# Block 1 of a PEER layer taken out ahead of blocks 2 and 3, and three weight loads put in front of the gather rows

## The chip, the cores and the metric

The kernel runs on one core of a Trainium2 chip. The metric is device microseconds of one execution. TensorE (PE) multiplies, VectorE (DVE) and ScalarE (ACT) work on elements, GpSimd (POOL) issues the indirect gathers, SyncE (SP) issues all plain loads and stores, and 16 DMA engines move the data.

## The reference

One decoder layer over 512 tokens of width 1024, in float32:

```python
z = x @ w_in      # q, fz, iv, og, cb, cc, ch, ga, gb, 1024 columns each
yc = cb * causal_depthwise_conv3(cc * ch, conv_w, conv_b)
merged = jax.nn.sigmoid(ga) * (o @ w_branch_a) + jax.nn.sigmoid(gb) * (yc @ w_branch_b)
x = layer_norm(ALPHA * x + merged @ w_out, ln1_g, ln1_b)
# peer(x): per token and head (8): product-key search, 16 experts of 16384
qh = (xb @ w_q).reshape(tb, PK_HEADS, 2, PK_HALF)
s = jnp.einsum('thpd,hpkd->thpk', qh, sub_keys)
s1, i1 = lax.top_k(s[:, :, 0], 16); s2, i2 = lax.top_k(s[:, :, 1], 16)
top, pos = lax.top_k(cand, 16)      # cand: the 256 sums of s1 and s2
h = gelu(einsum('thkd,td->thk', u[eidx], xb)); out = einsum('thk,thkd->td', softmax(top) * h, v[eidx])
x = layer_norm(ALPHA * x + out, ln2_g, ln2_b)
x = x + jax.nn.sigmoid(x @ ple_w_gate) * (p @ ple_w_proj)
```

Here o is a chunkwise gated recurrence over 8 heads. The 128 chosen experts of a token (8 heads by 16) are 8 KB each, u and v side by side.

## The kernel before, in words

The tokens are four blocks of 128. A first stage computes the recurrence for all of them and takes block 0 alone as far as its PEER queries. Then follow 512 **rows**, 128 to a block: row r gathers one expert of each of the 128 tokens (1 MB), VectorE multiplies its u half with x (dot, L1596), ScalarE makes the coefficient (gelu, softmax weight), and the v half is added with that coefficient, either by TensorE through a diagonal matrix into PSUM (`sum_v`, L2111) or, in the rows of the list SHARED, by VectorE (L1609). Six buffers `uv` hold gathered rows, a seventh is added from row MERGE_R to the end of block 0, two more from QUERY_R on. GpSimd issues the gather of a row when the row that had its buffer is summed.

The rest of the layer for blocks 1 to 3 is put into the rows of block 0 by tables of row numbers that each engine's program reads (`tail_row`):

- 40 **units** of 128 columns of x @ w_in (L2011; CHH, CC, CB for the convolution, GA, GB for the gates); two units share one 1 MB load, a pair. UNIT_ROW spreads them.
- 16 **merges** (L2030 and by VectorE L1358, L1363) with `w_branch_a` and `w_branch_b`, by MERGE_ROW.
- 12 **outs** (L2044, residual L1371) with `w_out`, by OUT_ROW, then the first norm of each block (L1378, L1385, L1395) by NORM_ROW and the transposes by TURN_ROW.
- the **queries** of 8 heads (L2078) and their **scores** (L2092), for blocks 1 to 3 in one product of 384 columns, by QUERY_ROW and SCORE_ROW.
- the **search** of an item (a block and a head, 15 steps on VectorE). Item i must be done before row 16 i is gathered. Item 8 is the first of block 1.

Every engine works through its own program in order; waits are on semaphores. Weights go by SP's queue, in order, into 1 MB slots: `raw` 0 to 3, `raw_w` 4 and 5. In the rows, units, merges and outs rotate over slots 0, 1, 2, and a load waits until the product that read its slot has ended. PSUM banks rotate over four for units and merges, so that TensorE can be four of them ahead of the engine that reads them.

A block's end (second norm, gate product L2161, projection L2176, store) runs in the rows of the next block, from FIN_TURN on. After row 511 comes a short tail.

Of the kernel before, what the change touches and what calls it, by code (L numbers as in the profile page):

```python
# [32 lines left out]
def build(nc, x, x_t, p_t, w_a, w_in, vec_cols, w_branch_a, w_branch_b, w_out,  # L33
# [21 lines left out]
    with ctx:  # L55
# [35 lines left out]
        def slot(i):  # L91

            if i < 4:
                return raw[:, i]
            if i < 6:
                return raw_w[:, i - 4]
            return raw_y[:, i - 6] if i < 8 else raw_g[:, i - 8]
# [132 lines left out]
        raw_in = [sem(f"raw_in{i}") for i in range(12)]  # L230
# [52 lines left out]
        def search_rows(i):  # L283

            if i == 1:
                return [k // 3 for k in range(STEPS)]
            if i == PKH:
                return [SCORE_ROW[0] + 2 + k // 2 for k in range(STEPS)]
            return [TOPK * (i - 2) + TOPK // 2 + k for k in range(STEPS)]

        UNITS = [(sect, 2 * cp + i) for cp in range(KT // 2) for sect in (6, 5, 4) for i in range(2)]
# [6 lines left out]
        UNIT_ROW += [[(UNIT_MM * n + i) * 58 // (UNIT_MM * (len(UNITS) - EARLY)) for i in range(UNIT_MM)]  # L298
                     for n in range(len(UNITS) - EARLY)]
        UNIT_ROW[EARLY] = [-1] + UNIT_ROW[EARLY][1:]  # L300
        UNIT_END = [rows[-1] for rows in UNIT_ROW]
        MERGE_ROW = [58 + n * 23 // 128 for n in range(16 * KT)]
        OUT_ROW = [83 + n * 11 // 96 for n in range(4 * (TB - 1) * KT)]
        NORM_ROW = [None] + [OUT_ROW[-1] + 1 + 2 * b for b in range(1, TB)]
        TURN_ROW = [None] + [NORM_ROW[b] + 3 for b in range(1, TB)]
        Q0 = TURN_ROW[-1] + 2
        QUERY_ROW = [[Q0 + (n * 5 // 16 if h == 0 else 6 + n * 6 // 16 if h == 1 else 17 + 14 * (h - 2) + n * 9 // 16)
                      for n in range(2 * KT)] for h in range(PKH)]
        SCORE_ROW = [QUERY_ROW[h][-1] + 2 for h in range(PKH)]

        SEARCH = [(i, search_rows(i)) for i in range(1, ITEMS)]

        def shared(r):

            b, k = divmod(r, BLOCK_ROWS)
            if b == 0:
                if r <= OUT_ROW[-1] + 3:
                    return True
                return r % 3 == 1 and 106 <= r <= 120
# [23 lines left out]
        MERGE_R, QUERY_R = BLOCK_ROWS - 2 - 5 * (UV + 1), QUERY_ROW[-1][-1] + 11  # L343
# [31 lines left out]
        FIN_TURN = 5  # L375
        FIN_GATE = [8 + n for n in range(2 * KT)]
        FIN_P = [FIN_GATE[-1] + 2 + n for n in range(4)]
# [43 lines left out]
        LOADS += [(("unit", n), n - 2 if n < 4 else (n - 2) % 3) for n in range(2, len(UNITS) // 2)]  # L421
        LOADS += [(("merge", m), m % 3) for m in range(8)]
        LOADS += [(("out", c), (c + 2) % 3) for c in range(4)]
        LOADS += [(("query", 1, h), h % 2) for h in range(PKH)]
# [7 lines left out]
        def blocks(pc):  # L432
            return range(*PIECES[pc])

# [40 lines left out]
        rest = [("merge", 1, c, i) for c in range(4) for i in range(4)]  # L475
        rest += [("out", 1, c, b) for c in range(4) for b in blocks(1)]
        rest += [("turn", 1, b, kh) for b in blocks(1) for kh in range(2)]
        for n, name in enumerate(rest):
            use(4 + (n + 2) % 4, *name)
        for h in range(PKH):  # L480
            for i in range(4):
                use(4 + i % 2, "query", 1, h, i)
# [42 lines left out]
        def chunk_end(m):  # L525
# [3 lines left out]
            return USE["out", 1, m - 8, TB - 1] + 1  # L529


        @block.sync
        def _(sp):
# [65 lines left out]
            sp.wait_ge(t_done, USE["unit", 1] + 1)  # L599
            unit_fetch(2)  # L600
            for h in (3, 4, 5):
                sp.wait_ge(t_done, USE["query", 0, h - 3, 1] + 1)
                fetch(pk_w_q[h], "query", 0, h)
            sp.wait_ge(t_done, USE["unit", 3] + 1)
            unit_fetch(3)
# [11 lines left out]
            for n in range(4, len(UNITS) // 2):  # L617
                if n == 4:
                    sp.wait_ge(t_done, USE["query", 0, 5, 1] + 1)
                elif n < 7:  # L620
                    sp.wait_ge(t_done, USE["unit", 2 * (n - 3) + 1] + 1)
                else:
                    sp.wait_ge(t_done, USE["unit", 2 * (n - 3) + 1] + 1)
# [6 lines left out]
            def tail_fetch(m, src, *name):  # L630
                if m < 3:
                    sp.wait_ge(t_done, USE["unit", len(UNITS) - 5 + 2 * m] + 1)
                else:
                    sp.wait_ge(t_done, chunk_end(m - 3))
# [7 lines left out]
            def query_fetch(h):  # L642
                if h < 2:
                    sp.wait_ge(t_done, chunk_end(9 + h))
                else:
                    sp.wait_ge(t_done, USE["query", 1, h - 2, 1] + 1)
# [10 lines left out]

            query_fetch(0)
            query_fetch(1)
            sp.wait_ge(t_done, chunk_end(11))  # L660
            sp.dma_start(w_ple[:], ple_w_proj).then_inc(ple_in, 16)

            sp.wait_ge(x1_done, TB)
            sp.dma_start(w_gate[:], ple_w_gate).then_inc(gate_in, 16)
            query_fetch(2)
            query_fetch(3)
# [58 lines left out]
        def _(act):  # L725
# [206 lines left out]
            def query_out(pc, h, parts=range(4)):  # L932
                bs = blocks(pc)
                n = P * len(bs)
                for i in parts:
# [3 lines left out]
                    o = qhT[pc][:, i, 0:n] if i < 2 else scores[:, i - 2, h, bs[0] * P:bs[0] * P + n]  # L939
# [54 lines left out]
            def tail_row(r):  # L994
# [13 lines left out]
                for h in range(PKH):  # L1008
                    for a in range(2):
                        if r == QUERY_ROW[h][KT * a + KT - 1] + 1:  # L1010
                            query_out(1, h, [a])
                    if r == SCORE_ROW[h] + 1:
                        query_out(1, h, [2, 3])
# [48 lines left out]
            for r in range(ROWS):  # L1062
# [8 lines left out]
                if b >= 0:  # L1071
                    if k == 2:
                        root_of(b, x2_var, x2_root)
                    if k == FIN_TURN + 1:
                        x2_turn_out(b)
                    if k == FIN_GATE[-1] + 1:
# [1266 lines left out]
```

## Time and profile before

| | us |
|---|---|
| median of 3 runs | 1784.62 (1783.69 to 1786.54) |
| the profiled execution, its own time | 1783.85 |
| its span | 1781.9 |
| TensorE busy | 1572.8 (88%) |
| VectorE busy | 1321.1 (74%) |
| ScalarE busy | 778.3 (44%) |
| GpSimd busy | 497.4 (28%) |
| DMA | 655.40 MB |

The profiled execution's time is 1.95 us more than its span, and 0.77 us less than the median. Busy time is a mean over stages with different limits, so it doesn't say by itself which engine a stage waits for; a page also divides the span into 40 slices of 44.5 us, and windows of the trace give the same for any stretch. DMA share is the busy share of the 16 DMA engines, and can read a little over 1.

### The profile page before, as it was taken

Reading aid. Unit: us, or ns where it says so; the run is one execution under the profiler, and the core shown is the slowest. Engines: PE = TensorE matmul, PEld = TensorE weight load, DVE = VectorE, ACT = ScalarE, POOL = GpSimd, SP = SyncE. Lnnn points to the kernel's source line nnn. Section 1 sums busy time; section 2 is a strip of 40 time slices with the busy share of each in tenths; the row PEclk is TensorE's granted clock in tenths of the full one; section 3 lists DMA queues with packets and bytes.
Section 4 is the critical chain, followed back from the end, with each engine's and each line's share of the span. In section 5 each row is a group of like instructions: output and inputs, shape, how many; then the busy total and the mean of one; then the engine's idle time right before and its main releaser. Section 6 shows DMA issues by size and latency. Waiting matters only on the chain. (4 is left out here: it accounts for less than half of the span.)

```text
span 1781.9 us, 16998 instructions
## 1 busy us (share of the span) xinstructions
PE 1572.8 (88%) x5000; PEld 874.4 (49%) x5000; DVE 1321.1 (74%) x2804; ACT 778.3 (44%) x1937; POOL 497.4 (28%) x528
## 2 busy tenths in 40 slices
PE   8999999999999997989888668788898878787778
PEld 7888888766655575544344223333333323222224
DVE  4454588599888999678878886886666687766666
ACT  6567695422222224343334334444444443444453
POOL 0000000122222232324333443333333333333331
PEclk9999999999999999999999999999999999999999
DMA  5113289799999999999999999999999999999994
GB/s 205 70 70 141 94 317 402 281 421 421 397 419 421 422 406 404 424 417 421 421 415 415 421 421 422 420 422 421 421 421 422 419 408 422 422 419 421 422 410 179
DMA packets 94933, 655.40 MB, mean 368 GB/s; under 512 B 10368, under 2 KB 14208, under 8 KB 17152
## 3 DMA queue, kind: packets, MB, share of 16 engines
q0 software_dynamic: 73728, 536.90, 72.8%
q1 hardware_dynamic: 20832, 116.97, 16.7%
q8 instruction: 37, 0.61, 0.1%
q10 hardware_dynamic: 288, 0.52, 0.1%
q14 instruction: 48, 0.39, 0.1%
HBM read 652.26 MB, written 2.10 MB: 367 GB/s over the span
## 5 line engine op out<-in xcount | busy, mean ns | idle before, releaser
L2111 PE MATMUL psum<-uv,diag 128*128 128x512 f32 x1424 | 707.3, 627 | 193.3 <-ACT diag L991 189.9
L720 POOL DMA_INDIRECT uv<-in_pk_uv,idx x512 | 495.0, 967 | 1249.6 <-PE psum L2111 563.9
L1596 DVE CUSTOM_DVE_ANT_0 uv<-uv,psum 128x1024 f32<-128x1024 f32 x512 | 622.9, 1217 | 295.1 <-DMA uv<-in_pk_uv,idx 288.0
L2111 PEld LDWEIGHTS psum<-uv,diag 128*128 128x128 f32 x1424 | 257.7, 194 | 613.2 <-ACT diag L991 389.7
L979 ACT ACTIVATE gelu<-dots 128x1 f32<-128x1 f32 x512 | 103.5, 202 | 764.1 <-DVE dots L1596 761.9
L2011 PE MATMUL psum<-xT,raw 128*128 128x384 f32 x640 | 208.4, 486 | 0.0
L1609 DVE SCALAR_TENSOR_TENSOR oT<-uv,coef,oT 128x1024 f32<-128x1024 f32 x151 | 193.3, 1280 | 4.2 <-ACT coef L983 4.2
L2011 PEld LDWEIGHTS psum<-xT,raw 128*128 128x128 f32 x640 | 120.7, 190 | 81.7
L983 ACT ACTIVATE coef<-gelu,weight 128x1 f32<-128x1 f32 x512 | 150.8, 295 | 16.6
L991 ACT ACTIVATE diag<-ident,coef 128x128 f32<-128x128 f32 x356 | 143.0, 402 | 11.6
L1847 PE MATMUL psum<-xTh,w_hi 128*128 128x512 f32 x248 | 98.6, 398 | 0.0
L1847 PE MATMUL psum<-xTl,w_hi 128*128 128x512 f32 x248 | 96.8, 390 | 0.0
L1847 PE MATMUL psum<-xTh,w_lo 128*128 128x512 f32 x248 | 96.5, 389 | 0.0
L2078 PE MATMUL psum<-oT,raw 128*128 128x384 f32 x256 | 92.2, 491 | 0.0
L1118 DVE TENSOR_TENSOR w_lo<-raw_a,w_hi 128x1024 fp32r<-128x1024 f32 x32 | 39.2, 1225 | 69.9 <-ACT w_hi L735 69.6
L2078 PEld LDWEIGHTS psum<-oT,raw 128*128 128x128 f32 x256 | 49.1, 192 | 45.6 <-issue 25.7
L1847 PEld LDWEIGHTS psum<-xTl,w_hi 128*128 128x128 f32 x248 | 46.5, 188 | 10.1
L1847 PEld LDWEIGHTS psum<-xTh,w_lo 128*128 128x128 f32 x248 | 46.6, 188 | 9.1
L1847 PEld LDWEIGHTS psum<-xTh,w_hi 128*128 128x128 f32 x248 | 46.6, 188 | 8.9
L2161 PE MATMUL psum<-w_gate,x2T 128*128 128x512 f32 x96 | 47.9, 592 | 0.0
L735 ACT ACTIVATE w_hi<-raw_a 128x1024 fp32r<-128x1024 f32 x32 | 34.0, 1061 | 31.3 <-PE psum L1847 27.9
L979 ACT ACT_TABLE_LOAD x35 | 44.9, 1283 | 0.6
(284 smaller groups left out, 1722.5 us busy)
## 6 DMA issues: line engine op xcount, KB each, us to landing
raw<-in_w_in SPq DMA_DIRECT2D x32, 1024.0 KB, 8.9
raw_a<-in_w_a SPq DMA_DIRECT2D x12, 1024.0 KB, 4.8
raw<-in_pk_w_q SPq DMA_DIRECT2D x10, 1024.0 KB, 9.5
raw_y<-in_w_in SPq DMA_DIRECT2D x8, 1024.0 KB, 6.8
raw<-in_w_branch_a SPq DMA_DIRECT2D x8, 1024.0 KB, 7.7
uv<-in_pk_uv,idx POOLq DMA_INDIRECT x512, 14.6
raw<-in_w_out SPq DMA_DIRECT2D x6, 1024.0 KB, 9.6
raw_w<-in_pk_w_q SPq DMA_DIRECT2D x6, 1024.0 KB, 9.5
```

Source lines behind the costliest of these rows:

```text
L720: pool.indirect_dma_start(row_uv(r)[:], None, pk_uv, bass.IndirectOffsetOnAxis(idx[:, i % 2, j:j + 1], 0)).then_inc(row_loaded(r)[0], 16)
L979: nc.scalar.activation(gelu[:, r % 4:r % 4 + 1], dots[:, r % 32:r % 32 + 1], ACT.Gelu).then_inc(gelu_done, 1)
L983: nc.scalar.activation(coef[:, r % 8:r % 8 + 1], gelu[:, r % 4:r % 4 + 1], ACT.Copy, scale=weight[:, i % 2, j:j + 1]).then_inc(coef_done, 1)
L991: nc.scalar.activation(diag[:, n % DR, :], ident[:], ACT.Copy, scale=coef[:, r % 8:r % 8 + 1]).then_inc(diag_done, 1)
L1118: V.tensor_tensor(w_lo[:, s], raw_a[:, slot, half], w_hi[:, s].bitcast(F32), ALU.subtract).then_inc(lo_done, 1)
L1596: V.tensor_tensor_reduce(u, u, x_cur[:], 1.0, 0.0, ALU.mult, ALU.add, dots[:, r % 32:r % 32 + 1]).then_inc(dot_done, 1)
L1609: V.scalar_tensor_tensor(out=acc, in0=v, scalar=c, in1=acc, op0=ALU.mult, op1=ALU.add).then_inc(acc_step, 1)
L1847: last = T.matmul(B[bk][:], w[:, s, k, :], xx[:, k, :], start=(k == 0 and i == 0), stop=(k == KT - 1 and i == 2))
L2011: last = T.matmul(B[bank(r)][:, 0:SEQ - P], slot(SLOT["unit", n // 2])[:, k, half * P:half * P + P], xT[:, k, P:], start=(k == 0), stop=(k ...
L2078: last = T.matmul(B[bank(r)][:, 0:n], w[:, k, a * P:a * P + P], turned[:, k, :], start=(k == 0), stop=(k == KT - 1), skip_group_check=True)
L2111: last = T.matmul(B[i][:], diag[:, n % DR, :], row_uv(r)[:, D + i * 512:D + (i + 1) * 512], start=(r in FIRST), stop=last_of_block, skip_g ...
L2161: last = T.matmul(B[6 + i][:], x2T[:, k, :], w_gate[:, k, i * 512:(i + 1) * 512], start=(k == 0), stop=(k == KT - 1), skip_group_check=True)
```

## The change

Five things are done in one edit. (1) Three slots, 12 to 14, are laid over columns that stand free for a time: those of blocks 2 and 3 in the first scores, and two blocks' columns in gaT and gbT. A load into such a slot is eight separate runs of 256 columns in each partition. Pairs 2, 3 and 4 are loaded there ahead of the rows, and slot 12 stays in the rotation to the end of outs. (2) Units take rows 0 to 67 where they took 0 to 57, merges 68 to 92 (58 to 80). (3) Outs are done for block 1 first, its norm in rows 101 to 103, then for blocks 2 and 3, with norms in rows 115 to 119; before, three norms stood in rows 96 to 102. (4) Queries 0 and 1 are computed for block 1 in rows 106 to 113 and for blocks 2 and 3 in rows 122 to 131; the other six stay joint. Item 8 is searched in rows 112 to 119 (113 to 120 before), item 10 in rows 143 to 150 (136 to 150). (5) SHARED has rows 0 to 112 in block 0 (0 to 96, 106, 109, 112, 115 and 118 before); the seventh buffer starts at row 105 (91); block 0's end starts 16 rows later.

```diff
+            if i >= 12:
+                return (scores[:, 0, :, 2 * P:], gaT[:, :, P:P + CW], gbT[:, :, P:P + CW])[i - 12]
...
             if i == PKH:
-                return [SCORE_ROW[0] + 2 + k // 2 for k in range(STEPS)]
+                return [SCORE_ROW[1, 0] + 2 + k // 2 for k in range(STEPS)]
+            if i == PKH + SPLIT:
+                return [SCORE_ROW[1, SPLIT] + 2 + k // 2 for k in range(STEPS)]
...
+        SPLIT = 2
+        MERGE0 = 68
-        UNIT_ROW += [[(UNIT_MM * n + i) * 58 // (UNIT_MM * (len(UNITS) - EARLY)) for i in range(UNIT_MM)]
+        UNIT_ROW += [[(UNIT_MM * n + i) * MERGE0 // (UNIT_MM * (len(UNITS) - EARLY)) for i in range(UNIT_MM)]
...
-        MERGE_ROW = [58 + n * 23 // 128 for n in range(16 * KT)]
+        MERGE_ROW = [MERGE0 + n * 25 // 128 for n in range(16 * KT)]
+        OUT0 = MERGE_ROW[-1] + 2
+        OUTS = [(c, 1) for c in range(4)] + [(c, b) for c in range(4) for b in range(2, TB)]
...
+        LATER = [(1, h) for h in range(SPLIT)] + [(2, h) for h in range(SPLIT)] + [(1, h) for h in range(SPLIT, PKH)]
...
-                if r <= OUT_ROW[-1] + 3:
-                    return True
-                return r % 3 == 1 and 106 <= r <= 120
+                return r <= OUT_ROW[-1]
...
-        MERGE_R, QUERY_R = BLOCK_ROWS - 2 - 5 * (UV + 1), QUERY_ROW[-1][-1] + 11
+        MERGE_R, QUERY_R = BLOCK_ROWS - 2 - 3 * (UV + 1), QUERY_ROW[1, PKH - 1][-1] + 11
...
-        FIN_TURN = 5
+        FIN_TURN = [21] + [5] * (TB - 1)
...
-        LOADS += [(("unit", n), n - 2 if n < 4 else (n - 2) % 3) for n in range(2, len(UNITS) // 2)]
-        LOADS += [(("merge", m), m % 3) for m in range(8)]
+        RING = (0, 1, 2, 12)
+        AHEAD = (12, 13, 14)
+        LOADS += [(("unit", n), (AHEAD + RING[:3] + AHEAD)[n - 2] if n < 11 else RING[(n - 11) % 4])
+                  for n in range(2, len(UNITS) // 2)]
+        LOADS += [(("merge", m), RING[(m + 1) % 4]) for m in range(8)]
...
             fetch(pk_w_q[2], "query", 0, 2)
-            sp.wait_ge(t_done, USE["unit", 1] + 1)
-            unit_fetch(2)
+            for n in range(2, 5):
+                unit_fetch(n)
             for h in (3, 4, 5):
                 sp.wait_ge(t_done, USE["query", 0, h - 3, 1] + 1)
                 fetch(pk_w_q[h], "query", 0, h)
+            sp.wait_ge(t_done, USE["unit", 1] + 1)
+            unit_fetch(5)
...
-            query_fetch(0)
-            query_fetch(1)
-            sp.wait_ge(t_done, chunk_end(11))
-            sp.dma_start(w_ple[:], ple_w_proj).then_inc(ple_in, 16)
-
+            for h in range(4):
+                query_fetch(h)
             sp.wait_ge(x1_done, TB)
             sp.dma_start(w_gate[:], ple_w_gate).then_inc(gate_in, 16)
-            query_fetch(2)
-            query_fetch(3)
+            sp.wait_ge(t_done, query_end(2, 1))
+            sp.dma_start(w_ple[:], ple_w_proj).then_inc(ple_in, 16)
             load_p(0)
```

On SP's queue the loads around the first gather stood like this before. keysT are the sub-keys, in_pk_w_q are query weights, in_w_in unit pairs, x2 two alike in a row; a load with 128x8x256 goes in runs of 256 columns.

```order
L597 DMA keysT<-in_sub_keys_t 128x2048 [waits zl_done]
L556 DMA raw<-in_pk_w_q 128x2048
L556 DMA raw<-in_w_in 128x2048 [waits t_done]
L556 DMA raw_w<-in_pk_w_q 128x2048 [waits t_done] x2
L556 DMA raw<-in_pk_w_q 128x2048 [waits t_done]
L556 DMA raw<-in_w_in 128x2048 [waits t_done]
```

In the changed kernel the same place of SP's queue reads:

```order
L632 DMA keysT<-in_sub_keys_t 128x2048 [waits zl_done]
L591 DMA raw<-in_pk_w_q 128x2048
L591 DMA scores<-in_w_in 128x8x256
L591 DMA gaT<-in_w_in 128x8x256
L591 DMA gbT<-in_w_in 128x8x256
L591 DMA raw_w<-in_pk_w_q 128x2048 [waits t_done] x2
L591 DMA raw<-in_pk_w_q 128x2048 [waits t_done]
L591 DMA raw<-in_w_in 128x2048 [waits t_done] x2
```

Three unit pairs have moved ahead of the waits on t_done, and the query loads no longer stand behind the wait for unit 1.

On VectorE, row 101 of the kernel before holds a dot (ISA, two instructions), one step of item 7's search (sel, weight), and the second step of block 3's first norm (BN_AGGR and the pass over x_sb).

```order
L1596 ISA uv_124,dots<-uv_124,psum 128x1024
L1596 ISA dots 128x1
L1509 TENSOR_REDUCE sel<-hot 128x16
L1511 TENSOR_REDUCE sel<-cand 128x16
L1515 TENSOR_SCALAR weight<-top_e,e_rec 128x16
L1383 BN_AGGR mean_var<-stats 128x2
L1385 SCALAR_TENSOR_TENSOR x_sb<-x_sb,mean_var,gaT 128x1024
```

The same norm step stands in row 118 of the changed kernel, behind two steps of item 8's search:

```order
L1629 ISA uv_123,dots<-uv_123,psum 128x1024
L1629 ISA dots 128x1
L1535 TENSOR_TENSOR hot<-hot,best_i 128x256
L1537 TENSOR_TENSOR cand<-cand,best_i 128x256
L1539 RECIPROCAL e_rec<-e_sum 128x1
L1542 TENSOR_REDUCE sel<-hot 128x16
L1544 TENSOR_REDUCE sel<-cand 128x16
L1548 TENSOR_SCALAR weight<-top_e,e_rec 128x16
L1416 BN_AGGR mean_var<-stats 128x2
L1418 SCALAR_TENSOR_TENSOR x_sb<-x_sb,mean_var,gaT 128x1024
```

The norms of blocks 2 and 3 have moved 17 rows later, from rows with one step of a search to rows with two.

## Rows read from the trace of the kernel before

**Rows 1.** The page: GB/s by slice, and the gathers' queue.
```profile
GB/s 205 70 70 141 94 317 402 281 421 421 397 419 421 422 406 404 424 417 421 421 415 415 421 421 422 420 422 421 421 421 422 419 408 422 422 419 421 422 410 179
...
q0 software_dynamic: 73728, 536.90, 72.8%
```

**Rows 2.** Windows: us, busy PE, PEld, DVE, ACT, POOL, PEclk, DMA share, GB/s.
```profile
345.00:455.00 110.00, 108.73 (x455) 72.07 (x454) 97.50 (x202) 27.93 (x98) 26.15 (x27) 1.00 1.01 419
455.00:475.00 20.00, 20.00 (x64) 11.79 (x63) 17.81 (x34) 3.18 (x13) 4.70 (x5) 1.00 0.97 378
475.00:645.00 170.00, 169.77 (x527) 99.72 (x525) 154.86 (x296) 42.43 (x132) 48.44 (x51) 1.00 1.01 421
645.00:705.00 60.00, 51.08 (x215) 40.32 (x216) 57.72 (x116) 19.62 (x50) 18.33 (x19) 0.97 1.01 410
705.00:730.00 25.00, 21.82 (x67) 10.89 (x66) 15.66 (x28) 11.87 (x31) 7.52 (x8) 1.00 0.97 396
```

**Rows 3.** Windows around the first gather, same columns.
```profile
326.00:336.00 10.00, 9.56 (x58) 7.51 (x57) 5.34 (x18) 4.04 (x12) 0.00 (x0) 1.00 0.04 16
336.00:342.00 6.00, 5.76 (x52) 5.60 (x51) 5.25 (x26) 2.32 (x5) 4.13 (x4) 1.00 0.96 363
```

**Rows 4.** Windows of rows 0 to 102, L1596 alone: busy us (two instructions a row).
```profile
347.40:541.00 193.60, 65.85 (x108) 1.00 1.01 415
541.00:641.30 100.30, 35.42 (x58) 1.00 1.01 421
641.30:679.50 38.20, 14.63 (x24) 1.00 1.00 403
679.50:711.40 31.90, 9.74 (x16) 0.95 0.99 406
```

**Rows 5.** Timeline of VectorE in rows 30, 88 and 98.
```profile
464.21 0.56 DVE L1329 TENSOR_TENSOR u_pad<-u_pad,psum 128x384 f32<-128x384 f32 x1 [2.11 <-PE psum L2011]
...
657.49 1.21 DVE L1596 CUSTOM_DVE_ANT_0 uv<-uv,psum 128x1024 f32<-128x1024 f32 x1
...
658.63 1.28 DVE L1609 SCALAR_TENSOR_TENSOR oT<-uv,coef,oT 128x1024 f32<-128x1024 f32 x1
659.83 0.48 DVE L1456 MAX8 best<-scores 128x8 f32<-128x128 f32 x2
660.23 0.40 DVE L1371 SCALAR_TENSOR_TENSOR x_sb<-x_sb,psum 128x256 f32<-128x256 f32 x1
660.55 1.21 DVE L1596 CUSTOM_DVE_ANT_0 uv<-uv,psum 128x1024 f32<-128x1024 f32 x1
...
695.16 1.28 DVE L1395 SCALAR_TENSOR_TENSOR x_sb<-x_sb,rstd,gbT 128x1024 f32<-128x1024 f32 x1
```

**Rows 6.** Timeline of SP's issues, of the first gather and the first dot.
```profile
335.31 0.33 SPq L556 DMA_DIRECT2D raw<-in_w_in  x1
335.68 4.17 SPq L556 DMA_DIRECT2D raw_w<-in_pk_w_q  x2
...
364.42 0.33 SPq L556 DMA_DIRECT2D raw<-in_w_in  x1
...
336.66 1.09 POOL L720 DMA_INDIRECT uv<-in_pk_uv,idx  x1 [333.40 <-DVE idx L1561]
...
347.43 1.22 DVE L1596 CUSTOM_DVE_ANT_0 uv<-uv,psum 128x1024 f32<-128x1024 f32 x1 [4.48 <-DMA uv<-in_pk_uv,idx]
```

**Rows 7.** Windows: xT alone (1.5 KB pieces), ln1 alone (512 B), gathers alone (8 KB).
```profile
296.00:298.00 2.00, 2.00 (x11) 1.65 (x10) 0.73 (x2) 1.10 (x2) 0.00 (x0) 1.00 1.06 372
309.00:311.00 2.00, 2.00 (x8) 1.18 (x7) 2.00 (x4) 0.33 (x1) 0.00 (x0) 1.00 1.18 292
1000.00:1200.00 200.00, 150.03 (x307) 56.16 (x308) 155.29 (x366) 83.61 (x251) 77.05 (x79) 0.96 1.01 421
```

**Rows 8.** DMA issues of 540:580 and of 700:712: size, median us to landing.
```profile
uv<-in_pk_uv,idx POOLq DMA_INDIRECT x12, 13.4
...
uv<-in_pk_uv,idx POOLq DMA_INDIRECT x3, 6.1
```

## What I expect, and why

> **What bounds the kernel now.** I read the page first, from the stage of rows to the end. From slice 9 to slice 39 the DMA moves 397 to 424 GB/s in every slice, and 536.90 MB of it are gathers [rows 1]. A row's gather is 1 MB: at the 421 GB/s of the stretch 1000 to 1200 us [rows 7] it takes 1.0486/421 = 2.49 us, and that is what a row costs where nothing else is loaded. The reader is to see that after 350 us the DMA engines are full nearly all the time, whatever VectorE or TensorE do, so the end moves only with (a) megabytes that leave the stage of rows, (b) megabytes that cost more, and (c) time in which the DMA runs dry.
>
> The second view, the windows of the stage, shows where it runs dry [rows 2]. What is lost in a window is its length times (421 - GB/s)/421: 0.5 us in 345:455, 2.0 us in 455:475, 0 in 475:645, 1.6 us in 645:705, 1.5 us in 705:730. The third view, windows of 326 to 342 us, shows the idle just ahead of the first gather: 16 GB/s from 326 to 336 [rows 3]. The fourth is what TensorE and VectorE did. L1596 counts two instructions a row, so 54 rows took 193.6 us (3.59 us each), the next 29 took 3.46 us, 12 rows 3.18 us and 8 rows 3.99 us [rows 4]. TensorE was busy for 108.73 of 110, 20.00 of 20 and 169.77 of 170 us up to 645 [rows 2]. VectorE waits for TensorE there too, 2.11 us at 464.21 [rows 5]. So in units and merges TensorE is level with the DMA, and at 455:475 it is behind.
>
> **Step 1, loads ahead of the rows (a gain).** Before, the load of unit pair 2 was issued at 335.31 and that of query 3 at 335.68; pair 3 came at 364.42 and pair 4 behind it [rows 6]. Now pairs 2, 3 and 4 are issued right behind query 2 with no wait, before the DMA falls idle at 326, and query 3, which stood behind a wait for unit 1, comes when query 0's product ends, about 332.3 us. The three take 9.0 us (step 2 has the rate), from 326.3 to about 335.3; query 3 follows to 337.8. Nothing of the rows waits for them: the first gather is issued at 336.66, when VectorE has its indices. But the windows say that 363 GB/s were moved from 336 to 342 before, 2.2 MB, which is pair 2 and query 3 [rows 3]: those two were hidden in part already. After the change the stretch from 337.8 to about 341 is nearly empty, since the gathers' own data come late (issued 336.66, the first used at 347.43 [rows 6]). So of four loads (4.19 MB, 10.0 us) some 1.6 MB is given back: 2.6 MB at 421 GB/s, **-6.2 us**. Ends: 4.9 us, if only pairs 3 and 4 count, and 7.5 us, if only one load's worth is given back.
>
> **Step 2, the new columns (a loss).** Slots 12 to 14 hold eight pieces of 256 columns a partition, not one run of 8 KB: each load into them is 1,024 pieces of 1 KB. Eleven loads go there, three ahead of the rows and eight among them (pairs 8, 9, 10, 14, 18, merges 2 and 6, out 2). The trace has no full load in 1 KB pieces, but xT goes in pieces of 1.5 KB and ran at 372 GB/s, the two vectors of ln1 in pieces of 512 B at 292 GB/s, against 421 for 8 KB [rows 7]. By these, 16 engines spend 66 ns on 1.5 KB and 28 ns on 512 B, so 47 ns on 1 KB: 349 GB/s, 3.00 us a load, 0.52 us more than 2.49. Eight of them: **+4.1 us**. Ends: 2.6 us (0.33 each, at 372) and 8.8 us (1.1 each, at 292); 1 KB is nearer to the first.
> The Trainium skill, "DMA: Bandwidth & Descriptors", its table at the head, gives 512 B or more as the size from which a transfer runs at line rate; by that rule this term would be 0. The rows disagree, 292 and 372 GB/s at a full DMA share, and I go by them.
>
> **Step 3, ten more rows for units and merges (a gain).** In 475:645 TensorE issues 527 instructions in 169.77 us [rows 2], nearly all halves of a product of 384 columns: 0.322 us each, 16 to a unit or a merge, 5.15 us. 38 units over 58 rows are 3.38 us a row, over 68 rows 2.88 us; 16 merges over 23 rows 3.58 us, over 25 rows 3.30 us. The DMA asks per row for 2.49 us of gather plus pairs: 18 over 58 rows was 3.26 us, now 15 over 68 (five of them at 3.00) is 3.08 us. So TensorE, which asked for more than the DMA before, asks for less. The wait of 2.11 us for a unit, and the 2.5 us lost in 345:475, should go: **-2.4 us** (ends 0 and 2.5). In these rows VectorE has 1.14 + 1.20 us of dot and sum, 0.5 of search (below) and less of the units' work than before; it stays under the DMA's 3.08.
>
> **Step 4, VectorE at the end of the block (no change taken).** Rows 97 to 105, 107, 108, 110 and 111 are now summed by VectorE, 115 and 118 by TensorE: 11 sums of 1.20 us more on VectorE. Its steps, from the pitches in the timeline [rows 5]: dot 1.14, sum 1.20, residual 0.32; a block's norm is three passes over 1,024 columns of 1.28 each and two short instructions, 4.1 us. 3.18 us a row of 641.3:679.5 less 1.14, 1.20 and 0.32 leaves 0.52 of search, 8.3 for an item's 16 rows. Rows 95 to 100: 6 x 3.18 = 19.1. Rows 101 to 103, with block 1's norm: 9.5 + 4.1 = 13.6. Rows 104 to 111, no search in them: 8 x 2.34 + 5 x 0.32 = 20.3. Rows 112 to 119, where item 8 is searched at two steps a row and the norms of blocks 2 and 3 stand as well: 8 dots, 2 sums, the item, 2 residuals, 2 norms, 9.1 + 2.4 + 8.3 + 0.6 + 8.2 = 28.6. Together 81.6 us for 25 rows. The DMA has 25 gathers and three query loads in that time, 62.2 + 7.4 = 69.6, because the 4 MB gate load now stands on SP behind query 3, which waits for row 125. VectorE is 12.0 us too slow. What covers it is the backlog: a gather takes a median 13.4 us from issue to landing at 540:580 and 6.1 us at 700:712 [rows 8], so some 7 us can be used up before the engines starve, and the seventh row buffer (from row 105) gives one more load, 2.5 us, and the wider pitch of rows itself holds more in flight. Before, the 8 rows with three norms did the same (31.9 us against 22.4 of DMA), and 1.6 + 1.5 us were lost. I take the same 3.1 us again: **0**. Ends: 2 us less, and 12.0 us more (no cover at all).
>
> **Step 5, the rest, at nothing.** Queries 0 and 1 are done for block 1 (128 columns) and again for blocks 2 and 3 (256): same columns, 32 more products, some 1.6 us of TensorE, behind a DMA that sets the pace of rows 106 to 133. Item 10 is searched in 8 rows, 143 to 150: 1.14 + 0.6 + 1.0 = 2.7 us against 2.49, 2 us in 8 rows, which the backlog covers. Block 0's last product moves 16 rows later, out of query 3 and into query 4's rows; store and query 7 follow it and are due at row 193. From there to slice 39 nothing changes: 408 to 422 GB/s by slice [rows 1]. The tail after the last row is the same code.
>
> **Sum.** -6.2 + 4.1 - 2.4 + 0 = -4.5 us. On the profiled execution's own 1783.85 that is 1779.4; the median shown, 1784.62, is 0.8 above it, and on that scale I predict 1780.1. A measurement tells about 0.2% (3.6 us) from no change, so this lies just outside.
>
> **Rivals.** (A) No measurable change: step 3's gain is not had, because idle follows late gathers elsewhere, or TensorE, now bound to the rows by four banks, waits in their place. -2.1, 1782.5. For it: the whole kernel lost only 6 us in this stage, and the net of steps 1 and 2 is small. (B) Slower: in rows 95 to 119 the DMA runs dry. Its price is 12.0 us less the cover c, so 1792.1 - c, and it ends over +0.2% where c is under 3.9 us, that is if the stretch is entered with the backlog already used up (gathers landing in under 10 us at row 95). Against it: the 13.6 us to 6.1 us of the rows before. (C) Pieces of 1 KB cost no more than 8 KB: step 2 falls away, -8.6 us, 1776.0. Against it the 372 GB/s. That is the page's rule named above. (D) The piece cost at its upper end, 8.8 us: +0.2, 1784.8, no change.
>
> **Numbers.** Forecast 0.44, C 0.08, A 0.28, D 0.05, B 0.15. So faster by over 0.2%: 0.52; within: 0.33; slower: 0.15. Range 1775 to 1788: from C's time and a little more, to B with 4 us of cover; what is beyond is under 2 in 10. The forecast's own range is 1777.5 to 1781.
>
> **What would show it.** Step 1: GB/s over 300 in 326:336, and fewer loads up to row 60. Step 2: GB/s under 421 at a full DMA share where a slot of scores, gaT or gbT is loaded. Step 3: 345:475 at 418 or more, TensorE's busy time under 100% in units. Step 4: gathers' time to landing not under 6 us in rows 95 to 125, and about 3 us lost there. I am wrong if that last stretch loses 6 us or more, or if TensorE's queue at the block's turn (queries of blocks 2 and 3 in rows 122 to 133) holds row buffers back.

## The result, and the profile after

The changed kernel takes 1800.09 us (median of 4 runs, 1798.33 to 1802.23), before 1785.53 beside it (1783.69 to 1786.54): ratio 1.008, 95% interval 1.0067 to 1.0092 (for the runs below the interval stands in brackets behind the ratio). It is 0.8% slower; I had said 1780.1 and 1775 to 1788. The span is 1796.4 against 1781.9, and 14.5 us is what has to be found.

The page of after, by slices of 44.9 us, beside [rows 1]:
```profile
span 1796.4 us, 17043 instructions
...
GB/s 211 69 62 140 108 324 397 352 417 410 414 416 417 416 415 379 400 354 355 421 380 421 422 420 423 420 422 421 421 422 421 422 393 421 421 421 421 421 418 185
```
The eighth slice (314 to 359 us) rises from 281 to 352; the 16th to 19th (674 to 853 us) and the 21st have 354 to 400, where before had 404 to 424. The gain is early; nearly all of the loss lies between 670 and 950 us. Windows of after (us, busy PE, PEld, DVE, ACT, POOL, PEclk, DMA share, GB/s), to set beside [rows 2, 3]:
```profile
326.00:336.00 10.00, 9.56 (x60) 7.73 (x59) 5.59 (x20) 4.04 (x12) 0.00 (x0) 1.00 1.08 362
336.00:342.00 6.00, 5.12 (x47) 4.96 (x46) 4.82 (x23) 2.08 (x5) 4.58 (x5) 1.00 0.93 342
345.00:475.00 130.00, 129.02 (x518) 84.34 (x519) 120.36 (x244) 35.87 (x123) 33.75 (x35) 1.00 1.02 415
475.00:645.00 170.00, 158.38 (x483) 91.71 (x482) 153.97 (x293) 40.05 (x130) 49.07 (x51) 0.99 1.02 416
645.00:705.00 60.00, 46.69 (x188) 36.08 (x187) 59.53 (x113) 14.25 (x42) 17.84 (x19) 0.89 1.00 392
705.00:780.00 75.00, 65.94 (x267) 43.48 (x266) 63.58 (x144) 34.35 (x97) 23.34 (x24) 0.98 0.99 397
780.00:860.00 80.00, 56.83 (x176) 32.14 (x175) 50.43 (x107) 27.18 (x78) 21.36 (x22) 0.85 0.88 352
860.00:950.00 90.00, 82.23 (x221) 39.89 (x221) 68.73 (x153) 34.54 (x104) 31.15 (x32) 0.98 0.99 401
950.00:1755.00 805.00, 650.61 (x1400) 250.85 (x1399) 584.61 (x1401) 349.99 (x1036) 309.02 (x321) 0.98 1.01 419
```
The same stretches of before, where [rows 2] doesn't have them:
```profile
296.00:345.00 49.00, 47.84 (x254) 38.28 (x253) 33.63 (x71) 24.33 (x43) 6.02 (x6) 1.00 0.76 282
345.00:475.00 130.00, 128.73 (x517) 83.86 (x516) 115.32 (x235) 31.12 (x110) 30.84 (x32) 1.00 1.01 413
...
705.00:780.00 75.00, 68.08 (x200) 34.63 (x199) 52.91 (x124) 32.42 (x92) 23.50 (x26) 0.98 1.00 413
780.00:860.00 80.00, 74.75 (x213) 37.19 (x212) 66.35 (x146) 34.94 (x100) 29.16 (x29) 1.00 1.01 419
860.00:950.00 90.00, 74.59 (x196) 36.88 (x195) 72.17 (x162) 34.63 (x106) 33.62 (x33) 0.92 1.01 414
950.00:1755.00 805.00, 647.74 (x1389) 247.97 (x1388) 579.93 (x1382) 350.55 (x1036) 305.07 (x318) 0.98 1.01 419
```
From 950 on the two are alike: all is decided before. The deepest hole is 780:860, and TensorE is idle there too (busy 56.83 of 80 us, at a granted clock of 0.85). The list of VectorE's waits names what is new in it; before, the third and fourth of these were 5.9 and 4.6 us, and the second didn't exist:
```profile
DVE uv L1629 <- DMA uv<-in_pk_uv,idx: 259.6, 304, 2.2
...
DVE rstd L1423 <- DMA ln_bias<-in_ln_b: 19.5, 1, 19.5
...
DVE uv L1629 <- ACT psum L1000: 13.9, 4, 10.1
DVE gate L1754 <- PE psum L2210: 10.2, 4, 5.5
```
VectorE's timeline around the 19.5 us: dot 132, then nothing until ln_bias has landed, then the second norm of block 0, then dot 133.
```profile
783.92 1.21 DVE L1629 CUSTOM_DVE_ANT_0 uv<-uv,psum 128x1024 f32<-128x1024 f32 x1
785.06 0.08 DVE L1629 DVE_READ_ACCUMULATOR2_ANT dots<- 128x1 f32 x1
804.65 0.16 DVE L1423 RECIPROCAL rstd<-rstd 128x1 f32<-128x1 f32 x1 [19.51 <-DMA ln_bias<-in_ln_b]
```
No row is summed in that time, so no buffer comes free, and GpSimd stands:
```profile
790.05 0.94 POOL L752 DMA_INDIRECT uv<-in_pk_uv,idx  x1 [3.68 <-PE psum L2145]
809.02 0.94 POOL L752 DMA_INDIRECT uv<-in_pk_uv,idx  x1 [18.03 <-DVE oT L1640]
```
Why is a 512 KB load late? SP's issues in the timeline of after (L702 is ln2_bias):
```profile
696.61 74.11 SPq L591 DMA_DIRECT2D raw<-in_pk_w_q  x4
770.76 0.43 SPq L696 DMA_DIRECT2D w_gate<-in_ple_w_gate  x1
791.53 0.33 SPq L698 DMA_DIRECT2D w_ple<-in_ple_w_proj  x1
791.91 0.43 SPq L691 DMA_DIRECT2D pT<-in_p_t  x1
792.38 0.43 SPq L702 DMA_DIRECT2D ln_bias<-in_ln_b  x1
```
The wait of SP that is new, in its list of waits (total, times, longest):
```profile
SPq L698 <- PE psum L2111: 20.3, 1, 20.3
```
SP's issues before:
```profile
711.54 0.33 SPq L664 DMA_DIRECT2D w_gate<-in_ple_w_gate  x1
733.92 21.58 SPq L556 DMA_DIRECT2D raw<-in_pk_w_q  x2
...
787.54 0.33 SPq L670 DMA_DIRECT2D ln_bias<-in_ln_b  x1
```
The change puts w_ple on SP behind a wait for query (2, 1), because its place is now query 1's slot. That query is 16 products in TensorE's stream of rows 128 to 131. It ends near 791, and ln2_bias, which waits only for block 0's sum, is queued behind it. Likewise the 4 MB of w_gate come 59 us later than before, behind query 3's wait for query (2, 0).

### The profile page after: what moved, and what is told of

The parts are those of the page before. It is cut to its first block and busy times, and to the rows that moved or that the text cites. A ratio compares the mean times of both kernels' runs of the same rounds, so it can differ in the third digit from the quotient of the medians.

```text
span 1796.4 us, 17043 instructions
## 1 busy us (share of the span) xinstructions
PE 1560.2 (87%) x5020; PEld 876.9 (49%) x5020; DVE 1332.5 (74%) x2815; ACT 773.8 (43%) x1934; POOL 497.1 (28%) x528
## 3 DMA queue, kind: packets, MB, share of 16 engines
q1 hardware_dynamic: 30688, 116.97, 16.9%
## 5 line engine op out<-in xcount | busy, mean ns | idle before, releaser
L2145 PE MATMUL psum<-uv,diag 128*128 128x512 f32 x1380 | 685.8, 627 | 196.1 <-ACT diag L1024 191.9
L2145 PEld LDWEIGHTS psum<-uv,diag 128*128 128x128 f32 x1380 | 248.5, 194 | 602.2 <-ACT diag L1024 390.5
L1642 DVE SCALAR_TENSOR_TENSOR oT<-uv,coef,oT 128x1024 f32<-128x1024 f32 x162 | 207.4, 1280 | 4.6 <-ACT coef L1016 4.6
L1024 ACT ACTIVATE diag<-ident,coef 128x128 f32<-128x128 f32 x345 | 138.5, 402 | 11.3
L2044 PE MATMUL psum<-xT,raw 128*128 128x384 f32 x384 | 127.6, 491 | 2.4 <-ACT gaT L955 2.4
L2044 PEld LDWEIGHTS psum<-xT,raw 128*128 128x128 f32 x384 | 73.1, 192 | 52.5 <-issue 4.9
L2111 PE MATMUL psum<-oT,raw 128*128 128x384 f32 (+2 forms) x320 | 91.5, 423 | 0.4 <-ACT scores L973 0.4
L2111 PEld LDWEIGHTS psum<-oT,raw 128*128 128x128 f32 x320 | 56.5, 191 | 39.7 <-issue 22.7
L2044 PE MATMUL psum<-xT,scores 128*128 128x384 f32 x128 | 42.7, 487 | 3.9 <-ACT gbT L955 3.9
```

Source lines behind the costliest of these rows:

```text
L1024: nc.scalar.activation(diag[:, n % DR, :], ident[:], ACT.Copy, scale=coef[:, r % 8:r % 8 + 1]).then_inc(diag_done, 1)
L1642: V.scalar_tensor_tensor(out=acc, in0=v, scalar=c, in1=acc, op0=ALU.mult, op1=ALU.add).then_inc(acc_step, 1)
L2044: last = T.matmul(B[bank(r)][:, 0:SEQ - P], slot(SLOT["unit", n // 2])[:, k, half * P:half * P + P], xT[:, k, P:], start=(k == 0), stop=(k ...
L2111: last = T.matmul(B[bank(r)][:, 0:n], w[:, k, a * P:a * P + P], turned[:, k, :], start=(k == 0), stop=(k == KT - 1), skip_group_check=True)
L2145: last = T.matmul(B[i][:], diag[:, n % DR, :], row_uv(r)[:, D + i * 512:D + (i + 1) * 512], start=(r in FIRST), stop=last_of_block, skip_g ...
```

## Experiments

Theory Q: the 14.5 us are SP's order at the block's turn. Rival T: they are TensorE's stream there (the split queries), and SP's order is a symptom.

**e1**, two items of SP exchanged:
```diff
+            sp.wait_ge(acc_out, 2)
+            sp.dma_start(ln2_bias[:], ln2_b[0].partition_broadcast(P)).then_inc(ln2_in, 16)
             sp.wait_ge(t_done, query_end(2, 1))
             sp.dma_start(w_ple[:], ple_w_proj).then_inc(ple_in, 16)
             load_p(0)
-            sp.wait_ge(acc_out, 2)
-            sp.dma_start(ln2_bias[:], ln2_b[0].partition_broadcast(P)).then_inc(ln2_in, 16)
```


> The changed kernel with two SP items exchanged: the wait for fin_sum(0) and the load of ln2_bias now stand ahead of the wait for query (2, 1) and the load of w_ple. Theory Q (SP's order): in the profile of after VectorE waits 19.5 us at row 132 for ln_bias, which lands at 804.6 because SP stood 20.3 us at the wait for query (2, 1); the wait vanishes, and the time falls from 1800.1 by 14 to 19 us, to 1781 to 1786. Rival T (TensorE's stream): what delays the block's turn is the 16 products of query (2, 1) in rows 128 to 131, and ln_bias was only the last of two late things; then the stall stays within a few us of where it is and the time is 1794 or more.

Measured 1787.84, ratio to before 1.0021 (1.0012 to 1.003), against after's 1.008: 0.59%, 10.5 us. T is out as the main cause, but Q as I put it was only part of it: I had said 14 to 19 us. The wait shrank from 19.5 to 11.0 us and didn't vanish; VectorE's and SP's timeline in e1:
```profile
795.06 0.16 DVE L1423 RECIPROCAL rstd<-rstd 128x1 f32<-128x1 f32 x1 [10.99 <-DMA ln_bias<-in_ln_b]
...
769.70 0.43 SPq L696 DMA_DIRECT2D w_gate<-in_ple_w_gate  x1
775.20 0.33 SPq L698 DMA_DIRECT2D ln_bias<-in_ln_b  x1
```
and its DMA issues (KB each, median us to landing):
```profile
w_gate<-in_ple_w_gate SPq DMA_DIRECT2D x1, 4096.0 KB, 21.6
...
ln_bias<-in_ln_b SPq DMA_DIRECT2D x1, 512.0 KB, 19.8
```
Issued 17 us earlier, it took 19.8 us to land (7.4 before), 5.5 us behind 4 MB of gate weights.

**e2**, the suspected cost alone, in the kernel before:
```diff
-            sp.wait_ge(t_done, chunk_end(11))
-            sp.dma_start(w_ple[:], ple_w_proj).then_inc(ple_in, 16)
...
             query_fetch(3)
+            sp.wait_ge(t_done, USE["query", 1, 2, 1] + 1)
+            sp.dma_start(w_ple[:], ple_w_proj).then_inc(ple_in, 16)
             load_p(0)
```


> The kernel before with the suspected cost alone put in: w_ple is loaded behind queries 2 and 3 and behind a wait for the end of the second half of query 2 (row 130), so that ln2_bias stands behind that wait too; nothing else is changed. Theory Q: in the profile of before ln_bias was issued at 787.5 and landed at 795.0, about when dot 132 began (794.9); row 130 is reached near 788 to 791, three small loads go first, and ln_bias lands at 800 to 804, which costs 4 to 9 us: 1789 to 1795. Rival T: SP's order there costs nothing by itself: 1785.5, within 2 us.

1793.88, ratio 1.0054 (1.0041 to 1.0068): 9.6 us (I had said 4 to 9) for w_ple moved behind three other loads and a wait, nothing else touched. Its rows, VectorE and SP:
```profile
807.68 0.16 DVE L1389 RECIPROCAL rstd<-rstd 128x1 f32<-128x1 f32 x1 [9.99 <-DMA ln_bias<-in_ln_b]
...
797.80 0.33 SPq L665 DMA_DIRECT2D w_ple<-in_ple_w_proj  x1
...
798.64 0.43 SPq L669 DMA_DIRECT2D ln_bias<-in_ln_b  x1
```

**e5**, e1 with the gate load ahead of query 3, and **e12**, after with this alone:
```diff
-            for h in range(4):
+            for h in range(3):
                 query_fetch(h)
             sp.wait_ge(x1_done, TB)
             sp.dma_start(w_gate[:], ple_w_gate).then_inc(gate_in, 16)
+            query_fetch(3)
```


> As e1 (1787.8), and the 4 MB load of w_gate stands ahead of query 3 on SP and not behind its wait for query (2, 0). In e1 w_gate was issued at 769.7 (before: 711.5) and ln_bias, issued 5.5 us behind it, took 19.8 us to land (before: 7.4), so that VectorE still waited 11.0 us for it at row 132. Theory G (the gate load's place): w_gate is issued near 745 to 750 and is over when ln_bias is issued at 775, which lands near 783; the 11.0 us go, and the time is 7 to 11 us under e1: 1777 to 1781, faster than before. Rival R (the lead cannot be kept): TensorE, which must finish its queue at the block's turn, makes VectorE wait in rows 128 to 172 for something else, and the time stays at 1785 or more.

> The changed kernel with only w_gate's load moved ahead of query 3; ln_bias still stands behind the wait for query (2, 1). Theory (the two placements are two stalls in series, the later one ends last): ln_bias is still issued near 792, and only its landing, 12.2 us after issue in after, gets shorter, to 7 to 9 us: 3 to 6 us under after, a ratio near 1.005. Rival: SP's two placements add, and it is 5 us better than after by itself and e1's 10 us more are independent; or it gives nothing, within 1.5 us of after (1.008).

e5: 1782.47, ratio 0.9988 (0.9979 to 0.9997), 0.33% or 5.9 us under e1 and just under before; I had expected 7 to 11. w_gate was issued at 749.3, ln_bias at 777.6, and the norm went on without a wait:
```profile
788.02 0.16 DVE L1424 RECIPROCAL rstd<-rstd 128x1 f32<-128x1 f32 x1
788.29 1.28 DVE L1429 SCALAR_TENSOR_TENSOR x<-x,rstd,ln_bias 128x1024 f32<-128x1024 f32 x1
```
e12: 1795.47, ratio 1.006, 3.6 us under after. ln2_bias, issued at 791.92, landed 8.7 us later and not 12.2, and VectorE waited 15.2 us for it and not 19.5. So moving the gate load gives 3.6 us where ln2_bias is still behind query (2, 1), and 5.9 where it isn't. Both make the same landing late: the wait by a late issue, the gate load in front by a long way from issue to landing.

**e3, e6, e7, e9**, the smaller waits of the block's turn. e3 is e1 with `FIN_TURN = [12]` for block 0. e6 is e5 with `or 121 <= r <= 126` in SHARED. e7 is e6, and e9 is e5, with fin_gate and fin_add three rows later (`FIN_P[b][2 * i + 1] + 4`, `FIN_P[b][3] + 5`).

> As e1, and the turn of block 0's gate at row 12 of block 1 and not 21, so that its gate's products stand in rows 143 to 158 and the four of w_ple in rows 160 to 163, between queries 4 and 5, and no longer in rows 169 to 172 beside query 5's. Theory: the 5.5 us at row 172 that VectorE waits for the product of w_ple are a loss of their own and go: 3 to 5 us under e1. Rival: row buffers or a later wait take them back, and the time is e1's within 1.5 us.

> As e5, and the six rows 121 to 126 are summed by VectorE and not by TensorE (6 x 1.72 us off TensorE's stream, 6 x 1.20 us onto VectorE's). In e1 dot 128 waited 9.0 us for ScalarE's copy of block 1's tokens, which stood behind the copy of query (2, 0), whose products TensorE reached 5 us late. Theory: that wait falls to under 2 us and half of it or more is kept: 3 to 6 us under e5. Rival: row buffers come free no earlier, the lead is bounded by the transfers, and the time is e5's within 1.5 us; or VectorE, at 2.9 us a row there, is slower than the 2.5 us in which a row arrives, and it is 1 to 3 us over e5.

> As e6, and VectorE's products of the gate with the projection (fin_gate, fin_add) stand three rows later in each block, so that VectorE goes on with dots where it stood 5.4 us in row 172 of e1 for the last product of w_ple. Theory: TensorE is late there only against VectorE's order, and 3 to 5 us go. Rival: TensorE is late by its own load in rows 150 to 173 (two gates' products, queries 4 and 5), row buffers wait for its sums instead, and the time is e6's within 1.5 us.

> As e5 (ratio 0.9988 to before), with fin_gate and fin_add three rows later in each block and without the six more shared rows of e6. In e5 dots fell back by 5.0 us against before at row 172, where VectorE waits for the product of w_ple. Theory: 1.5 to 4 us under e5 (1779 to 1781). Rival: e7 kept only 1.6 us of these 5, since row buffers then waited for TensorE's sums in rows 176 to 185, and so it is here: within 1.5 us of e5.

e3: 1787.6, ratio 1.0016 against e1's 1.0021: the rival. The wait moved to row 162 (6.11 us, for the same product). e6: 1785.11, 0.9999, 2.0 us over e5: the rival again. In e6 GpSimd stood 10.29 us for a sum of TensorE ahead of its gather at 781.14, and 780:860 moves 399 GB/s where e5 moves 419. e7: 1783.06, 0.999, 1.6 us under e6, just past its rival's 1.5 where the theory wanted 3 to 5. e9: 1782.06, 0.9985 (0.9976 to 0.9994), 0.5 us under e5, the rival. Dot 172 of e7 stands 6.4 us ahead of e6's and dot 185 only 1.8, since GpSimd waited for TensorE's sums between them. Four edits at the places where VectorE is seen to wait, and none worth 2 us. What I read from this, and no run shows by itself: in rows 140 to 185 TensorE holds this schedule (81 to 82 of 90 us busy in 860:950 in after and e5, 74.59 before, since block 0's products stand there), and who is seen to wait for it is only a matter of order.

**e4, e10, e14, e15**, what made the early lead. e4 is before with the three loads ahead, pair 5 on over the old three slots:
```diff
-        LOADS += [(("unit", n), n - 2 if n < 4 else (n - 2) % 3) for n in range(2, len(UNITS) // 2)]
+        LOADS += [(("unit", n), n + 10 if n < 5 else (n - 5) % 3) for n in range(2, len(UNITS) // 2)]
...
-            sp.wait_ge(t_done, USE["unit", 1] + 1)
-            unit_fetch(2)
+            for n in range(2, 5):
+                unit_fetch(n)
```
e10 is e4 with the change's AHEAD and RING. e14 has the rows of e5 (MERGE0 = 68, split queries) with no load ahead and three slots, out 3 alone in slot 12; e15 is e14 with the three loads ahead. Both also wait at the block's turn in another order than e5 (w_ple behind query (2, 0), and query 3 behind w_ple and query (2, 1)), so they are set against e5 up to 705 us only.

> The kernel before with only the three unit pairs loaded ahead of the rows, into the same places in 1 KB pieces (pairs 2 to 4); from pair 5 on a ring of the three old slots, the unit, merge and output rows as before, queries not split. By the forecast's first step it is 6.2 us faster less three loads' share of the 1 KB pieces (3 of 11, 1.1 us): 1780.4. By the trace of after, where row 0 came 3.9 us earlier: 1781.6. Rival: a lead at row 0 is given back where VectorE and not the DMA sets the pace (rows 95 to 119), and it ends within 1.5 us of before, 1784 to 1787.

> The kernel before with the three loads ahead and the change's ring of four places (the fourth a column of first scores) and six places for pairs 5 to 10, but none of the rest: units, merge and output rows, queries of three blocks, block 0's gate and SP's order at the block's turn as before. Theory M (the lead is made by loads and ring, and lost by the new order at the block's turn): dot 33 is 6 to 10 us earlier than in before, as in e5, and with SP's old order the lead stays: 4 to 8 us under before, a ratio of 0.9955 to 0.998. Rival N (the longer rows for units made the lead): TensorE or VectorE holds rows 8 to 58 at their old pace, as in e4, and it is within 2 us of before.

> The other half of e10: no unit pair loaded ahead and the old ring of three places (the fourth output chunk alone stands in the free column of first scores, since the new output order needs four at once), but unit, merge and output rows, the split queries and the order of e5 as in e5. Theory P (the loads make room and the longer rows let it be used: neither alone gives the lead): dot 33 stands within 2 us of before and the time is at or over before, 1784 to 1789. Rival N (the longer rows made the lead by themselves, since TensorE was busy 160.00 of 160 us in 400:560 of before): dot 33 is 4 us or more earlier, and the time is e5's within 2 us.

> As e14, with the three pairs loaded ahead again (into the columns, 1 KB pieces), so that it is e5 without the ring's fourth place and without pairs 8 to 10, 14 and 18 in columns. Against e14 it prices the three loads where rows are long enough to use them; against e5 the deeper ring with its 1 KB pieces. Theory P: 3 to 7 us under e14. If pieces of 1 KB cost 0.8 us a pair, as e8 against e7 says (7.1 us for 9), then the five pairs and three chunks that return to 8 KB rows save 4 to 6 us and it is faster than e5, 1776 to 1779; if the depth of the ring is what kept the DMA busy, it is slower than e5, 1784 or more.

e4: 1784.24, ratio 0.9998, its rival's time, but the lead was gone by 475 us and not in rows 95 to 119. e10: 1784.42, 1.0 (0.9991 to 1.0009), rival N. e14: 1788.72, 1.0021 (1.0012 to 1.003), the time of theory P, but dot 33 at 464.2 us, 8.5 earlier than before (472.6), as rival N has it. e15: 1786.34, 1.0008 (0.9999 to 1.0017), 2.3 us under e14 where theory P wanted 3 to 7, and 3.6 over e5. Dots don't show a lead well, since a row's place says nothing of the weights still unloaded. Bytes do: the window's length times the difference in GB/s, summed from 296 us. In MB over before (0.42 MB are 1 us; a unit of GB/s is 0.05 to 0.17 MB in a window, and 0.8 in the last, which is left out):

| MB over before at | 345 | 475 | 645 | 705 | 780 | 860 | 950 | span, us |
|---|---|---|---|---|---|---|---|---|
| after | 2.9 | 3.2 | 2.4 | 1.3 | 0.1 | -5.3 | -6.5 | +14.5 |
| e1 | 3.1 | 3.4 | 2.5 | 1.6 | -0.1 | -0.9 | -1.9 | +2.7 |
| e5 | 3.0 | 3.2 | 2.3 | 1.7 | 1.4 | 1.4 | 0.3 | -2.2 |
| e4, loads | 3.1 | 0.1 | 0.1 | -0.1 | -0.4 | -0.5 | -0.9 | +1.0 |
| e10, loads and ring | 3.0 | 2.9 | 0.9 | 0.2 | -0.4 | -0.8 | -1.0 | +1.0 |
| e14, rows | 0.0 | 1.0 | 0.9 | -0.9 | -1.2 | -1.0 | -2.1 | +3.8 |
| e15, loads and rows | 3.1 | 2.3 | 2.3 | 0.2 | -0.4 | -0.2 | -1.6 | +2.5 |

The windows of e4 and e14 on which this rests:
```profile
400.00:475.00 75.00, 75.00 (x281) 47.47 (x280) 66.20 (x127) 16.17 (x60) 18.74 (x20) 1.00 0.96 367
```
```profile
345.00:475.00 130.00, 128.79 (x516) 83.92 (x515) 120.30 (x246) 34.72 (x120) 33.97 (x35) 1.00 1.01 421
475.00:645.00 170.00, 157.69 (x476) 90.03 (x476) 154.27 (x292) 39.84 (x129) 48.69 (x51) 0.99 1.01 420
645.00:705.00 60.00, 42.07 (x150) 30.91 (x149) 54.65 (x106) 13.90 (x40) 15.95 (x18) 0.83 0.94 380
```
In e4 the loads bring 3 MB ahead, and TensorE, 75.00 of 75 us busy, gives the DMA 367 GB/s until they are gone. The longer rows take TensorE off the path (157.69 of 170) and make 1 MB by themselves; only with them are the 3 MB kept (e15: 2.3 at 645). In 645:705, where outs begin, every kernel with the new rows loses against before: with three slots 1.8 and 2.2 MB, with four 0.6 to 1.1. So the fourth place earns what its columns cost: e5 and e15 are level at 645 (e5 has paid for 1 KB pieces, e15 for the DMA's dip to 397 GB/s in 400:475), and 1.5 MB apart at 705. With three places the last weights of outs come late, and TensorE stands for them in e15 (4.92 us in e14), VectorE for TensorE (6.93 us), GpSimd for VectorE (10.87 us):
```profile
688.27 6.72 PE L2075 MATMUL psum<-scores,gaT 128*128 128x256 f32 x16 [5.82 <-DMA scores<-in_w_out]
```

**e8**, every unit pair in 1 KB pieces, in e7's schedule:
```diff
-                fetch(w_in[sect - CB, c // 2], "unit", n)
+                for odd in range(2):
+                    sp.dma_start(dst.rearrange("p (a b) n -> p b a n", b=2)[:, odd],
+                                 src.rearrange("p (a b) n -> p b a n", b=2)[:, odd]).then_inc(raw_in[SLOT["unit", n]], 16)
```


> As e7, and every unit pair, in whichever place it lands, is loaded as two halves of 1 KB pieces; the pairs that already had them are 11 of 20, so 9 more do. It doubles the suspected cost of the change's second step. By that step (8 KB rows at 421 GB/s, 1 KB pieces as bounded there: 0.37 us a pair) it costs 3.3 us over e7. Rival: pieces of 1 KB cost nothing, since two DMAs of 512 KB are taken up beside the gathers, and it is within 1 us of e7.

1790.13, ratio 1.0032 (1.0021 to 1.0043) against e7's 0.999: 7.5 us by the ratios, 7.1 by the medians. I had counted wrong: of the change's eleven loads in 1 KB pieces eight are pairs and three are not (merges 2 and 6, out 2), so the edit adds twelve pairs, not nine. The page has it: 41,760 packets on SP's queue against 30,688, 11,072 more, which is 896 for each of twelve pairs (e4 has 2,688 more than before for its three) and 320 for the 20 more issues. That is 0.6 us a pair, and not 0.8 as I took it in e15's expectation; nor is 0.37 step 2's price, which is 0.52 and would give 6.2 us. Windows of e7 and of e8, both at a DMA share over 1:
```profile
475.00:645.00 170.00, 161.63 (x483) 93.41 (x482) 155.01 (x294) 40.04 (x130) 48.12 (x51) 0.97 1.02 417
```
```profile
475.00:645.00 170.00, 150.36 (x446) 87.18 (x445) 148.48 (x283) 38.73 (x126) 47.58 (x50) 0.94 1.02 408
```
Not all of it is the bare price of pieces. A pair in slot 12 came late, TensorE stood 12.64 us for it, and GpSimd issued nothing for 15.27 us; in 526:543 e8 moves 0.9 MB less than e7, 2.2 us.
```profile
525.03 13.66 PE L2048 MATMUL psum<-xT,scores 128*128 128x384 f32 x32 [12.64 <-DMA scores<-in_w_in]
...
536.13 0.93 POOL L756 DMA_INDIRECT uv<-in_pk_uv,idx  x1 [15.27 <-DVE oT L1646]
```
And e8 splits each pair into two loads of 512 KB as well. What pieces cost without either can be read in after, where for 6 us the queue holds little else: of 2092 packets 2091 are under 2 KB, and at a DMA share of 1.10 they move 353 GB/s (the window, then the line of its packets).
```profile
328.00:334.00 6.00, 5.76 (x37) 4.82 (x37) 3.03 (x10) 2.19 (x7) 0.00 (x0) 1.00 1.10 353
DMA packets 2092, 2.12 MB, mean 353 GB/s; under 512 B 32, under 2 KB 2091, under 8 KB 2091
```

## Why the prediction was wrong

**Step 1 was right in size, and rests on step 3.** I had 2.6 MB; 2.9 MB were ahead at 345 us (7.0 us), with 362 GB/s in 326:336 against 16. What I hadn't seen is that it is worth nothing by itself (e4, e10). TensorE at 108.73, 20.00 and 169.77 us of its windows stood in [rows 2], and I wrote that it was level with the DMA, but not what follows: a lead of the DMA can't be kept while TensorE sets the pace.

**Step 2 was right, in its price and in its sum.** I had 349 GB/s for 1 KB pieces and 4.1 us for eight loads; pieces by themselves moved 353. In 345:475 e5 moves 414 GB/s and e14 421, in 475:645 416 and 420: 0.9 + 0.7 MB, or 3.8 us (a unit of GB/s is 0.3 to 0.4 us here), for the seven of the eight that fall there: 0.54 us each, where I had 0.52. Rival C, free pieces, is refuted by 415 GB/s at a share of 1.02 where whole rows run at 421 with 1.01, by the 353, and by e8. The Trainium skill, "DMA: Bandwidth & Descriptors", table at the head, has 512 B as the size from which a transfer runs at line rate; here neither 1 KB (353 GB/s) nor 1.5 KB (372 [rows 7]) does, against 421 for whole rows, and the measurement decides.

**Step 3 was right.** 2.4 us forecast; e14 has 0.9 MB by 645, 2.1 us, and TensorE at 157.69 of 170. The three steps together were to give 4.5 us near the end of merges; after is 2.4 MB, 5.6 us, ahead there. Up to 645 us the forecast holds.

**Step 4 took 0 where some 3 us were lost, within its ends.** Rows 95 to 119, in before and in after:
```profile
679.56:760.14 80.58, 67.19 (x219) 37.10 (x218) 63.09 (x134) 39.68 (x98) 25.20 (x26) 0.98 1.00 413
```
```profile
669.58:749.59 80.01, 67.51 (x305) 53.28 (x306) 79.41 (x156) 32.45 (x85) 25.21 (x26) 0.93 0.99 397
```
I had 81.6 us of VectorE for these 25 rows, and they took 80.0 with VectorE busy for 79.41. Against 421 GB/s they lose 4.6 us, where before lost 1.5: more than the 3 I took, less than the 6 that would have refuted the step. Rival B's dry spell, up to 12 us, didn't come (gathers took a median 10.0 us to land in 700:712, more than the 6.1 of before [rows 8]). Its real fault is another: it books the late gate load as 4 MB that rows 95 to 119 are spared, and doesn't ask where they go next.

**Step 5 is where it failed: "the rest, at nothing".** It looked at block 0's last product, store and query 7, and not at what else is queued on SP behind the two new waits. ln2_bias behind the wait for query (2, 1), and w_gate behind the wait for (2, 0), cost 19.5 us of waiting at row 132. Put right, they give back 10.5 us (e1) and 5.9 us (e5), 16.4 together, more than the 14.5 us lost; and e2 makes 9.6 us by the first of the two in a kernel that has nothing else of the change. That is the step that failed. Before, the slack was small: ln_bias, issued at 787.54, landed 7.4 us later, at 794.9, and the norm took it at 796.3, 1.4 us after. In after the norm was ready at 785.1, 11 us earlier, and the load was issued 4.8 us later. The step had a second hole: between 860 and 950 us, where block 0's products are moved to, after, e5, e14 and e15 all lose 1.1 to 1.4 MB (2.6 to 3.2 us) with TensorE at 79 to 82 us of 90; that TensorE makes the loss there is read, not tested. Of those rows I had costed item 10's search, on VectorE, and not TensorE.

**The last sentence of the prediction** named TensorE's queue at the block's turn. It is there: ScalarE waited 5.31 and 4.80 us for query (2, 0) ahead of row 128, so that dot 128 waited 10.1 us for ScalarE's copy of block 1's tokens. What it costs depends on what else is to be loaded. In after and e1 only gathers were left, and 705:780 loses 1.2 and 1.7 MB; in e5 the gate load fills just that time, and 0.3 MB are lost: the wait for the copy reads 1.70 us, and three rows earlier VectorE waits 8.09 us for a gather instead. e6, which works on it there, gains nothing.

**What stays open.** That VectorE makes 645:705 lose 0.6 to 1.1 MB was read from its busy time (59.53 of 60 us); TensorE is busy for 20.00 of 20 us in 685:705 as well, and no run relieved either there. Nor did a run relieve TensorE in rows 150 to 172. And e8 does not separate a second issue from what pieces cost beside gathers.

The lowest of these kernels is e9, ratio 0.9985 (0.9976 to 0.9994), not told apart from e5's 0.9988: 2.7 us under before and some 17 under the change. The change's idea carries 5.5 us to 645 us (e5, 2.3 MB), and what follows, up to 950 us, takes more than half of it back.

## What to carry to other kernels

When an edit adds a wait to an in-order DMA queue, write down every load behind it, with the slack between its landing and its use in the trace of before: 1.4 us on a 512 KB load decided this case, not the eleven loads that were rearranged. Also ask of a large load that is moved later what will be issued just behind it. And count a lead in bytes, not in steps of the loop: after was 18 us ahead by dots at row 127 and level with before by bytes at 780 us, since at that row w_gate (4 MB), w_ple and query 3 (1 MB each), some 15 us of transfer, were still to come, which before had already.

## What the hardware showed that I had not expected

- A 512 KB load issued 5.5 us behind a 4 MB one on the same queue landed 19.8 us after issue, 3.7 us behind the 4 MB (e1: 769.70 + 21.6 and 775.20 + 19.8); without it in front it took 7.4 us (before).
- Loads in 1 KB pieces cost throughput at a full DMA share, as I had estimated (353 GB/s against 421 for 8 KB rows), and they also take long to land beside gathers: a median 25.3 and 25.8 us in 475:645 of after, where loads in whole rows took 9.1 to 9.7 in the same stretch of before. How much of that is the deeper rotation of slots, no run here tells apart.
- The granted clock followed the stall. In after TensorE waited 17.63 us before its product at 809.13; the clock read 1.00 (2.4 GHz) in 785:790, 0.88 in 790:795, 0.50 (1.2 GHz) in 795:810, and 1.00 again from 815. In 780:860 that makes 0.85, where e5, without the stall, has 1.00.
```profile
795.00:800.00 5.00, 0.00 (x0) 0.00 (x0) 0.00 (x0) 0.00 (x0) 0.00 (x0) 0.50 1.01 419
```
